# A mixture of experts in order of load: four experts with 128 places, then four with 64 places and two weight slots streamed side by side

## The reference, cut to what matters

```
def moe_swiglu(t, router, w_gate, w_up, w_down):      # t: 256 x 1024
    logits = t @ router                                # 8 experts
    top_logits, top_idx = lax.top_k(logits, 2)
    gates = softmax(top_logits)
    combine = sum(one_hot(top_idx, 8) * gates[..., None], axis=1)
    for e in range(8):                                 # hidden width 3584
        out += combine[:, e:e+1] * (silu(t @ w_gate[e]) * (t @ w_up[e])) @ w_down[e]
```

## Time and profile before

| | us |
|---|---|
| median of 3 runs (3666.02, 3676.64, 3676.02) | 3676.02 |
| the profiled execution | 3665.99 |
| its span | 3664.2 |
| TensorE (matmuls) busy | 3445.9 (94%) |
| VectorE busy | 909.2 (25%) |
| ScalarE busy | 486.7 (13%) |
| mean granted TensorE clock | 0.971 of full |
| data moved | 635.84 MB, mean 174 GB/s |

### The profile page before, as it was taken

The page is one execution under the profiler, slowest core; times in us unless marked ns, Lnnn a source line. Parts: engine busy times, 40 slices in busy tenths (PEclk is TensorE's granted clock), DMA queues, the critical chain, the costliest instruction groups (busy, mean ns, idle before and its releaser), DMA issues.

```text
span 3664.2 us, 44945 instructions
## 1 busy us (share of the span) xinstructions
PE 3445.9 (94%) x18488; PEld 2561.9 (70%) x18515; DVE 909.2 (25%) x1893; ACT 486.7 (13%) x1139; POOL 106.7 (3%) x115
## 2 busy tenths in 40 slices
PE   7999987999999988996879999899999999999998
PEld 4565666577776765775756768578888888888876
DVE  1677777300101331004750002210010100001001
ACT  1322231000100220002121012200000000000000
POOL 0121120000000000000000000000000000000000
PEclk9999998999999999998989999899999999999999
DMA  6444411345445213432003453268888888888885
GB/s 212 150 163 176 145 54 47 125 149 162 137 149 172 75 58 123 153 112 93 35 23 127 160 161 88 80 226 285 287 273 295 271 288 286 270 295 271 296 275 196
DMA packets 474963, 635.84 MB, mean 174 GB/s; under 512 B 11094, under 2 KB 419261, under 8 KB 467525
## 3 DMA queue, kind: packets, MB, share of 16 engines
q1 hardware_dynamic: 469645, 612.49, 50.5%
q0 software_dynamic: 5184, 21.46, 1.8%
HBM read 632.70 MB, written 1.20 MB: 173 GB/s over the span
## 4 chain that ended last, share of the span: by engine, by line
PE 84%; DVE 6%; DVEq 2%; issue 2%; DMA 2%; ACT 2%; PEld 1%; PEldq 1%; ACTq 0%; SPq 0%; POOL 0%
PE PS L714 38%; PE PS L722 19%; PE PS L1067 4%; PE PS L2937 2%; PE PS L537 2%; PE PS L1621 1%; PE PS L1617 1%; DMA WO<-in_ada_w 1%; PE PS L1875 1%; DVE scratch L1466 1%; PE PS L1196 1%; PE PS L276 1%; PE PS L3262 1%; PEld PS L537 1%; PE PS L2949 1%
## 5 line engine op out<-in xcount | busy, mean ns | idle before, releaser
L741 DVE TENSOR_TENSOR scratch<-scratch,PS 128x128 f32<-128x128 f32 (+1 forms) x312 | 101.5, 325 | 1965.3 <-ACT scratch L731 1964.8
L714 PEld LDWEIGHTS PS<-scratch,WO 128*128 128x128 f32 x3584 | 417.8, 192 | 53.6 <-issue 53.6
L714 PEld LDWEIGHTS PS<-scratch,WF 128*128 128x128 f32 x3584 | 409.0, 192 | 24.1 <-issue 23.0
L714 PE MATMUL PS<-scratch,WO 128*128 128x128 f32 x3584 | 418.2, 275 | 0.0
L714 PE MATMUL PS<-scratch,WF 128*128 128x128 f32 x3584 | 409.2, 275 | 0.0
L722 PE MATMUL PS<-WF,scratch 128*128 128x512 f32 x816 | 374.9, 592 | 0.0
L731 ACT ACTIVATE scratch<-PS 128x128 f32<-128x128 f32 (+1 forms) x312 | 96.0, 308 | 1966.0 <-PE PS L714 1966.0
L722 PE MATMUL PS<-WO,scratch 128*128 128x512 f32 x784 | 350.0, 592 | 0.0
L714 PE MATMUL PS<-XT,WF 128*128 128x256 f32 x1472 | 324.6, 381 | 1.7 <-ACT XT L482 1.7
L714 PEld LDWEIGHTS PS<-XT,WF 128*128 128x128 f32 x1472 | 280.9, 191 | 51.5 <-issue 12.0
L714 PE MATMUL PS<-XT,WO 128*128 128x256 f32 x1344 | 296.0, 379 | 0.0
(11 more groups left out here) (526 smaller groups left out, 3081.0 us busy)
## 6 DMA issues: line engine op xcount, KB each, us to landing
WF<-in_moe_wg SPq DMA_DIRECT2D x56, 1024.0 KB, 5.1
WF<-in_moe_wu SPq DMA_DIRECT2D x56, 1024.0 KB, 7.6
WF<-in_moe_wd SPq DMA_DIRECT2D x56, 1024.0 KB, 4.9
WO<-in_moe_wg SPq DMA_DIRECT2D x56, 1024.0 KB, 5.1
WO<-in_moe_wu SPq DMA_DIRECT2D x56, 1024.0 KB, 7.6
WO<-in_moe_wd SPq DMA_DIRECT2D x56, 1024.0 KB, 7.2
WO<-in_ada_w SPq DMA_DIRECT2D x48, 1024.0 KB, 6.4
WF<-in_ffn_w_gate SPq DMA_DIRECT2D x17, 1024.0 KB, 5.4
```

What stands on the lines that cost most here:

```text
L714: mm = nc.tensor.matmul(k.PS[:, 4 + f, w * n:(w + 1) * n], slot.gu[:, w, kb, f * P:(f + 1) * P], rhs(kb), start=kb == 0, stop=kb == KB - 1)
L741: k.nc.vector.tensor_tensor(hid[:, f, :], sg[:, f, :], k.PS[:, 4 + f, n:2 * n], ALU.mult).then_inc(*slots[s].dve.done(f"h{f}"))
```

## The change

The experts are taken by rank of load, found on the chip. The four fuller ones ("many") go through turns as before. The four emptier ones ("few") have 64 places. There the roles in "up" are swapped: 64 columns of tokens are the stationary operand and 256 columns of weights move, and slot 0 and slot 1 are used in alternate matmuls, whose results lie in partitions 0 to 63 and 64 to 127 of one bank. "Down" alternates in the same way. Two transposes bring the hidden values from rows to columns. There are four weight slots in place of two: turns alternate between the pair (WF, WO) and a new pair (XT, OT and scratch). `load_round` is unchanged. The second pass would run if one of the four fuller has over 128 tokens or one of the others over 64. The core of the diff:

```diff
 def router_vector(k, dve):
...
+    dve.wait_ge(*k.rt_pe.at("places"))
+    stt(k.load, k.PS[:, 6, 16:24], float(EXPERTS), k.slot_iota[:, 0:EXPERTS], ALU.mult, ALU.subtract)
...
+    nc.vector.max(k.loads_down, k.load)
...
+    nc.vector.max_index(k.order.bitcast(U32), k.loads_down, k.load)
...
+    dve.drain().then_inc(*k.rt_dve.done("order"))
...    (places of each expert sorted by rank: 4 products of 128x64, 4 sums)
+    dve.drain().then_inc(*k.rt_dve.done("ranked"))

+def expert_turn(k, i, t):
+    n = i * E_TURNS + t
+    base = MOE_BASE if n % 2 == 0 else (0, 0)
+    return k.expert_slots[2 * (n % 2):2 * (n % 2) + 2], [n // 2 + b for b in base]

+def moe_sync(k, sp):
+    ups, downs = expert_weights(k)
+    sp.wait_ge(*k.rt_dve.at("order"))
+    sp.wait_ge(*k.rt_pe.at("logits"))
+    for i, rank in enumerate(RANKS):
+        e = sp.value_load(k.order[0:1, rank:rank + 1].bitcast(I32), min_val=0, max_val=EXPERTS - 1)
+        for turn in range(E_TURNS):
+            slots, rnds = expert_turn(k, i, turn)
+            for s in range(2):
...
+                load_round(k, sp, slots[s], rnds[s], *gu, dn)

+def few_up_tensor(k, pe, i, turn, ws):
+    slots, rnds = expert_turn(k, i, turn)
+    bank = few_bank(i, turn)
+    if ws[0] == 0:
+        for s in range(2):
+            pe.wait_ge(slots[s].gu_in, (rnds[s] + 1) * 32)
+    for w in ws:
+        for kb in range(KB):
+            for s in range(2):
+                mm = k.nc.tensor.matmul(k.PS[ROWS[s], bank, w * ROUND:(w + 1) * ROUND],
+                                        k.xte[:, i % 2, kb, s * FEW:(s + 1) * FEW], slots[s].gu[:, w, kb, :],
+                                        start=kb == 0, stop=kb == KB - 1)
+                if kb == KB - 1 and w:
+                    mm.then_inc(*slots[s].pe.both("up0", "up1"))

+def few_flip_tensor(k, pe, i, turn):
...    (waits for the products of both slots, then 2 transposes of 128x128)

+def few_down_tensor(k, pe, i, turn):
...    (waits for both slots' down weights and for ScalarE's copy of the flip)
+    for f in range(2):
+        for half in range(2):
+            for s in range(2):
+                mm = k.nc.tensor.matmul(k.PS[ROWS[s], acc + half, :], k.few_ht[:, f, s * FEW:(s + 1) * FEW],
+                                        slots[s].dn[:, f, half * 512:(half + 1) * 512], start=False, stop=False)
+                if f and half:
+                    mm.then_inc(*slots[s].pe.both("down0", "down1"))

+def few_tensor(k, pe, i):
+    acc = (2 * (i % 2), 2 * (i % 2) + 1)
+    zero_sum(k, True, acc)
+    few_up_tensor(k, pe, i, 0, range(2))
+    scatter_tensor(k, pe, i - 1, 0)
+    for turn in range(E_TURNS):
+        if turn + 1 < E_TURNS:
+            few_up_tensor(k, pe, i, turn + 1, (0,))
+        few_flip_tensor(k, pe, i, turn)
+        if turn + 1 < E_TURNS:
+            few_up_tensor(k, pe, i, turn + 1, (1,))
+        elif i + 1 < EXPERTS:
+            gates_turn_tensor(k, pe, i + 1)
+        few_down_tensor(k, pe, i, turn)
+        if turn == 0:
+            scatter_tensor(k, pe, i - 1, 1)
+        if turn == E_TURNS - 2 and i + 1 < EXPERTS:
+            gather_tensor(k, pe, i + 1)
+    zero_sum(k, False, acc).then_inc(*k.sc_pe.done("acc"))
```

More of the change, by code:

```diff
@@ L129, in at, with both @@
         return self.sem, rnd * self.n + (self.n + self.names.index(name) + 1)
+    def both(self, first, second):
+        self.done(first)
+        return self.done(second)[0], 2
     def done(self, name):
@@ L3134, in declare_moe @@
     k.rt_act = Steps(k, "rt_act", "gates")
[L3135 to L3138, removed]
+    k.rt_dve = Steps(k, "rt_dve", "top chosen order places ranked")
+    k.ga_pe = Steps(k, "ga_pe", "ga tr")
+    k.ga_act = Steps(k, "ga_act", "ga tr")
+    k.ga_dve = Steps(k, "ga_dve", "g")
+    k.sc_pe = Steps(k, "sc_pe", "acc sc0 sc1")
+    k.sc_dve = Steps(k, "sc_dve", "y x0 x1")
+    k.few_pe = Steps(k, "few_pe", "flip")
+    k.few_act = Steps(k, "few_act", "flip")
+    xt, ot = (b.rearrange("p a b -> p (a b)") for b in (k.XT, k.OT))
+    third = Slot(k, "third", xt[:, 0:UPS], ot[:, 0:DOWNS])
+    fourth = Slot(k, "fourth", k.S[:, 12288:12288 + UPS], ot[:, DOWNS:2 * DOWNS])
+    k.expert_slots = [*k.dense, third, fourth]
     k.rw_ = view(k, 6144, KB, 8)
@@ new lines, in router_vector @@
+    nc.vector.tensor_copy(k.counts, k.PS[:, 6, 16:24]).then_inc(*k.rt_dve.done("places"))
+    ts(k.route[:, 0, :, 0:EXPERTS], k.lg, -1.0, None, ALU.add)
+    tt(k.of_rank, bcast(k.load, EXPERTS), k.loads_down.unsqueeze(2).to_broadcast([P, EXPERTS, EXPERTS]), ALU.is_equal)
+    ts(k.many, k.load, k.loads_down[:, MANY_RANKS - 1:MANY_RANKS], None, ALU.is_ge)
+    dve.drain()
+    route = k.route.rearrange("p a t e -> p (a t) e")
+    for n in range(4):
+        tt(k.picked[:, n, :, :], bcast(route[:, n, 0:EXPERTS], EXPERTS), k.of_rank, ALU.mult)
@@ L3235, in router_vector @@
+    stt(k.over_, k.many, float(FEW - SLOTS), k.counts, ALU.mult, ALU.add)
+    ts(k.caps, k.many, float(SLOTS - FEW), float(FEW), ALU.mult, ALU.add)
+    dve.drain()
+    for n in range(4):
+        nc.vector.reduce_sum(k.ranked[:, n, :], k.picked[:, n, :, :], AX)
+    nc.vector.reduce_max(k.most, k.over_, AX)
+    dve.drain()
+    ts(k.most, k.most, float(SLOTS - FEW), None, ALU.add)
     dve.drain()
     nc.vector.tensor_copy(k.flag.bitcast(I32), k.most)
-    dve.drain().then_inc(*k.rt_dve.done("places"))
@@ L3244, in moe_sync, with more_sync @@
+def more_sync(k, sp):
+    ups, downs = expert_weights(k)
+    base = [b + PAIR_ROUNDS for b in MOE_BASE]
     with sp.Fori(0, EXPERTS) as e:
@@ L3293, in moe_tensor, with more_tensor @@
+def moe_tensor(k, pe):
+    gather_tensor(k, pe, 0)
+    gates_turn_tensor(k, pe, 0)
+    for i, rank in enumerate(RANKS):
+        if rank < MANY_RANKS:
+            many_tensor(k, pe, i)
+        else:
+            few_tensor(k, pe, i)
+    for tile in range(2):
+        scatter_tensor(k, pe, EXPERTS - 1, tile)
+def more_tensor(k, pe):
+    base = [b + PAIR_ROUNDS for b in MOE_BASE]
+    gather_tensor(k, pe, EXPERTS)
+    gates_turn_tensor(k, pe, EXPERTS)
     for e in range(EXPERTS):
-        u, first, last = e % 2, e * E_TURNS, (e + 1) * E_TURNS - 1
+        u, i, first, last = e % 2, EXPERTS + e, e * E_TURNS, (e + 1) * E_TURNS - 1
@@ L3364, in moe_vector @@
-def moe_vector(k, dve, sweep, base, first):
-    route = k.route.rearrange("p a t e -> p (a t) e")
-    last_b = lambda rnd: (lambda f: sweep.slots[1].pe.at(f"down{f}", rnd + (base[1] - 1)))
-    choice_vector(k, dve, 0, route[:, :, 0:1], first).then_inc(*sweep.ga_dve.done("g"))
+        nc.vector.tensor_scalar(k.ge_[:, u, tile, :], places, pos, None, ALU.is_equal)
+        nc.vector.tensor_scalar(k.gated[:, u, tile, :], places, pos, gate, ALU.is_equal, ALU.mult)
+    dve.drain().then_inc(*k.ga_dve.done("g"))
@@ new lines, in many_vector @@
+def many_vector(k, dve, i):
+    for turn in range(E_TURNS):
+        slots, rnds = expert_turn(k, i, turn)
+        before, at = expert_turn(k, i, turn - 1) if turn else expert_turn(k, i - 1, E_TURNS - 1) if i else (slots, [r - 1 for r in rnds])
+        last = lambda f: before[1].pe.at(f"down{f}", at[1])
+        for s in range(2):
+            turn_vector(k, dve, slots, (s,), rnds, SLOTS, k.sgm, k.hidm, last)
+            if turn == 0 and i:
+                scatter_vector(k, dve, i - 1, s)
+        if turn == 0 and i + 1 < EXPERTS:
+            rank_vector(k, dve, i + 1)
@@ new lines, in few_vector @@
+def few_vector(k, dve, i):
+    for turn in range(E_TURNS):
+        slots, rnds = expert_turn(k, i, turn)
+        bank = few_bank(i, turn)
+        if few_round(i, turn):
+            dve.wait_ge(*k.few_pe.at("flip", few_round(i, turn) - 1))
+        for s in range(2):
+            dve.wait_ge(*slots[s].act.at("silu1", rnds[s]))
+            k.nc.vector.tensor_tensor(k.few_h[ROWS[s], :], k.few_sg[ROWS[s], :], k.PS[ROWS[s], bank, ROUND:2 * ROUND],
+                                      ALU.mult).then_inc(*slots[s].dve.both("h0", "h1"))
+        if turn < 2:
+            scatter_vector(k, dve, i - 1, turn)
+        if turn == 1 and i + 1 < EXPERTS:
+            rank_vector(k, dve, i + 1)
@@ new lines, in moe_vector, with more_vector @@
+def moe_vector(k, dve):
+    rank_vector(k, dve, 0)
+    for i, rank in enumerate(RANKS):
+        if rank < MANY_RANKS:
+            many_vector(k, dve, i)
+        else:
+            few_vector(k, dve, i)
+        sum_vector(k, dve, i)
+    for tile in range(2):
+        scatter_vector(k, dve, EXPERTS - 1, tile)
+def more_vector(k, dve):
+    base = [b + PAIR_ROUNDS for b in MOE_BASE]
+    route = k.route.rearrange("p a t e -> p (a t) e")
+    last_b = lambda rnd: (lambda f: k.dense[1].pe.at(f"down{f}", rnd + (base[1] - 1)))
+    for tile in range(2):
+        k.nc.vector.tensor_tensor(route[:, tile, 0:EXPERTS], route[:, tile, 0:EXPERTS], k.caps, ALU.subtract)
+    dve.drain()
+    choice_vector(k, dve, EXPERTS, route[:, :, 0:1], k.slot_iota)
@@ L3377, in moe_vector @@
         with dve.Fori(1, E_TURNS) as j:
```

(3 more changed lines are left out.)

259 lines of the change are left out of this document (159 added, 100 removed).

## The result

| | before | changed |
|---|---|---|
| median of 12 runs, us | 3673.99 (3662.98 to 3676.64) | 3682.7 (3671.22 to 3688.96) |
| ratio | | 1.0025, 95% interval 1.0014 to 1.0037 |
| span of the profiled execution, us | 3664.2 | 3680.8 |
| TensorE busy | 3445.9 | 3209.7 |
| mean granted clock | 0.971 | 0.933 |

TensorE works 236 us less, and the kernel takes 9 us more (5 to 14 by the interval). The forecast was 3717 with a range of 3650 to 3790. The direction and the order of waits came out as written, the size was four to five times too large, because two terms of TensorE's burst were too long.

What follows compares the result with a forecast made beforehand. TensorE was taken to bound the kernel, loads close behind. From 3665.99 us, start -0.8 and emptier experts +48.6 gave 3713.8, and a third of the runs' 10 us spread made the median 3717; range 3650 to 3790.

Steps and rivals of the forecast that it cites:

- the order of waits: Emptier experts: SyncE's loads wait for "down", queued behind TensorE's wait for weights; transfer and work alternate, 23.1 us per turn.
- TensorE's burst: Emptier experts' up, flip and down per turn: 11.7 us at full clock, against 21.16 before; 11.1 by a full 2x.
- What bounds, and the limit of 17.4 us per turn: Experts' turns: TensorE bounds at 21.16 us, loads close behind at 17.4, so a turn can gain at most 3.8 us.
- The fuller experts, 0 us: The four fuller experts: same matmuls in the same order, bound by TensorE before and after, so no change.
- Idle from burst to burst: Emptier experts: TensorE waits 0.24 us for issue, 11.0 for three MB to land and 0.18 to start.
- The clock: Emptier experts: the granted clock falls in TensorE's idle gaps, costing 2.6 us per burst; interval 25.7 us.
- my lower bound of 24.4: Low end, in us, of the range for one long interval in the emptier experts, 24.4 to 28.0.
- The sign: Whole kernel: slower, chance 0.70; emptier experts 669.6 us against 621.0, +48.6 us.
- The start: Before the experts: ranking adds 3.9 us, the router starts 4.7 us earlier; sum -0.8 us, range -5 to +6.
- the clock staying up (3657): Rival: clock stays at 1.00 through the gaps, 22 intervals and last burst each lose 2.6 us less; chance 0.12.
- Prefetch that works (3525): Rival: emptier experts' loads run ahead and DMA engines bound every turn at 17.4 us; chance 0.11.
- Tiles not beside each other: Rival: tiles don't run beside each other at 256 or 512 columns, or clock stays low; 3923 us, chance 0.08.

Runs made afterwards that it cites:

- e1: Changed kernel with SyncE issuing gate and up weights of both slots first, then both down weights, in the emptier experts: 3519.45 us, ratio 0.9583 to the kernel before.
- e4: Changed kernel with TensorE doing flip and "down" of a turn before "up" of the next, SyncE unchanged: 3521.8 us, ratio 0.9593 to the kernel before.
- e2: Changed kernel with 44 bfloat16 matmuls of zeros behind "down" of turns 0 to 4 of each emptier expert: 3666.7 us, ratio 0.9994 to the kernel before.
- e3: Changed kernel with all of slot 0's matmuls before slot 1's, in "up" and "down" of the emptier experts: 3799.84 us (one run).

## Why the prediction was right and wrong

- **What bounds, and the limit of 17.4 us per turn**: right. Most turns of e1 and e4 take 17.0 to 17.3, at 365 GB/s.
- **The fuller experts, 0 us**: right, 156.21 us each.
- **The order of waits**: right in each step. 22 long and 3 short intervals; the wait in load_round stands in SyncE's waits; e1 and e4 show that it is the cause. Idle from burst to burst was forecast as 11.4 us and is 11.4 on average where nothing but the burst lies in the interval.
- **TensorE's burst: the term that failed.** I gave a pair of tiles 0.465 us, by the 0.03 that L2133 loses with 128 columns. With 256 columns nothing is lost: neighbours start 0.43 us apart per pair, and "down" pairs 0.86 apart. With the clock at 1.00 a burst is 11.1 us (e1: from 3043.83 until TensorE runs dry at 3054.91), not 11.7. The Trainium skill, TensorEngine Tiling (Array Packing), section Theoretical Speedup, gives up to 2x. With 256 and 512 moving columns this trace agrees with the full 2x, and the 11.1 us that the prediction worked out for that case is what was measured.
- **The clock, the second term that failed.** Forecast 2.6 us per burst, from a gather that took 2.9 longer. It is 1.6 on average: the 16 bursts with nothing else in their interval take 12.65 us, against 11.1 at clock 1.00. The very first lost 2.6, the one in which the clock rose after 4.3 us lost 2.1, most others 1.3 to 1.5. Together the two terms are 0.6 and 1.0, that is 1.6 us too much per interval, 22 times 35 us, and the last burst 2: 669.6 forecast, 632.0 measured. The measured 24.1 lies even under my lower bound of 24.4, because I had not put all the lowest values (11.0, 2.0, 10.6) together; they give 24.0. Over 22 intervals, two terms that were 5% and 60% too large made a loss of 48.6 us out of one of 10.9.
- **The sign**: the emptier experts lost 10.9 us, 0.5 per long interval. That is less than either of the two errors (0.6 and 1.0). "Slower" followed from the right mechanism, but that it held by so little owes something to luck.
- **The start**: forecast -0.8, measured -2.2. From the residual addition to the router's first matmul are 8.6 us in place of 12.7, a gain of 4.1 (forecast 4.7); the rest up to the first "up" takes 1.9 us more (forecast 3.9).
- **The rivals**: the clock staying up (3657) is refuted for the changed kernel, and e2 shows what it would have given. Prefetch that works (3525) is what e1 made of it, 3519. Tiles not beside each other: refuted by the 0.43 us per pair; e3 shows the price of a queue that doesn't alternate. The time I gave this rival, 3923, had left out the clock, which by the forecast's own 2.6 us per burst would have added some 60.

## What to carry to other kernels

More buffers are not more prefetch. Write down for each load which instruction must end before it can be *issued*, in the issuing engine's own queue order, and then what stands in front of that instruction on its engine; if the chain comes back to the load itself, buffers don't help, and swapping two statements may. Where one interval repeats 22 times, an error of 0.5 us in each term decides between 0.3% and 1%: take such terms from the row nearest in shape, and forecast with the sum of the lowest as well.

## What the runs showed of the hardware

- Two 64-column tiles with alternating instructions lose nothing at 256 and 512 moving columns (0.43 us per pair of float32 matmuls with 256 columns, the time of one on the full array), but 14% at 128 columns (0.255 against 0.223).
- With the matmuls of one tile in a row before those of the other, the tiles overlapped only over a few neighbouring records at each change, and bursts grew from about 12.8 to 19.6 us (e3).
- A transfer of 64 KB that GpSimd issued took 7.5 us to land beside six loads of SyncE, and 3.4 us with none.
- Matmuls of zeros in bfloat16 in the waits held the granted clock at 1.00 in all but three of the bursts behind them (e2).
